# A layer's adaLN projection moved from TensorE to VectorE and TensorE together, and a bias table written in eight copies

## What is computed

```python
cond_act = jax.nn.silu(cond)
for i in range(DEPTH):
    mod = (cond_act @ ada_w[i] + ada_b[i])[:, None, :]      # ada_w[i]: 1024 x 6144
    sh1, sc1, g1, sh2, sc2, g2 = [mod[..., n * D:(n + 1) * D] for n in range(6)]
    h = rms_norm(x, norm1_g[i]) * (1 + sc1) + sh1
    # m = pool_mix / attention / fourier_mix of h
    x = x + g1 * m
    h = rms_norm(x, norm2_g[i]) * (1 + sc2) + sh2
    x = x + g2 * moe(h, ...)
```

## Time and profile before

| what | value |
|---|---|
| median of 3 runs | 1320.46 us |
| lowest and highest run | 1318.17, 1323.54 us |
| the profiled execution | 1320.7 us, of which the span is 1318.9 us |
| TensorE busy | 1247.3 us (95%) |
| VectorE busy | 392.1 us (30%) |
| ScalarE busy | 332.1 us (25%) |
| moved by DMA | 535.45 MB, 406 GB/s over the span |
| granted TensorE clock, mean | 0.983 |

### The profile page before, as it was taken

How to read it: one execution, slowest core, us unless ns; L and a number is a source line. 1 busy time by engine, 2 the same in 40 slices (tenths; PEclk the granted TensorE clock), 3 DMA queues, 4 the chain that set the end, 5 groups by cost and what they waited for, 6 DMA issues and landing times.

```text
span 1318.9 us, 17286 instructions
## 1 busy us (share of the span) xinstructions
PE 1247.3 (95%) x6581; PEld 563.0 (43%) x6581; DVE 392.1 (30%) x884; ACT 332.1 (25%) x714; POOL 37.7 (3%) x76
## 2 busy tenths in 40 slices
PE   3879999999899999999999899999999989999996
PEld 0434434343756644443434354443443454434342
DVE  1242213222232324221332324222231452213324
ACT  1141212122221223221212233221221452212122
POOL 2100000000200000000100000000000000000000
PEclk9879999999999999999999999999999999999998
DMA  9999999999999988999999999999999999999994
GB/s 371 420 420 421 421 421 421 421 420 421 398 368 409 394 335 360 422 421 421 420 420 421 421 407 399 422 421 421 420 421 421 415 421 418 422 420 420 422 420 182
DMA packets 87279, 535.45 MB, mean 406 GB/s; under 512 B 11192, under 2 KB 13336, under 8 KB 25760
## 3 DMA queue, kind: packets, MB, share of 16 engines
q1 hardware_dynamic: 82336, 527.47, 97.3%
q0 software_dynamic: 3120, 5.17, 1.1%
q10 hardware_dynamic: 1744, 1.73, 0.4%
HBM read 532.20 MB, written 2.12 MB: 405 GB/s over the span
## 4 chain that ended last, share of the span: by engine, by line
PE 86%; DMA 7%; DVE 4%; ACT 2%; issue 1%; SPq 0%; DVEq 0%; ACTq 0%
PE ps L1939 33%; PE ps L1988 15%; PE ps L1925 5%; PE ps L2000 5%; PE ps L1614 4%; PE ps L1451 4%; PE ps L1576 4%; DMA ring<-in_ada_w_dram 4%; PE ps L1971 3%; PE ps L1623 2%; DMA ring<-in_attn_wqkv_dram 2%; DMA ring<-in_moe_w_down_dram 2%; PE ps L1956 1%; PE ps L1548 1%; ACT hT L707 1%; PE ps L1485 1%
## 5 line engine op out<-in xcount | busy, mean ns | idle before, releaser
L1941 PE MATMUL ps<-ring,xg 128*64 128x512 f32 x968 | 438.0, 597 | 0.0
L1939 PE MATMUL ps<-ring,xg 128*64 128x512 f32 x912 | 412.5, 597 | 2.8 <-DMA ring<-in_moe_w_up_dram 2.8
L1988 PE MATMUL ps<-ring,gb 128*64 128x512 f32 x992 | 225.6, 595 | 0.3 <-DMA ring<-in_moe_w_down_dram 0.3
L1939 PEld LDWEIGHTS ps<-ring,xg 128*64 128x64 f32 x912 | 117.5, 137 | 228.4 <-issue 218.7
L1375 DVE SCALAR_TENSOR_TENSOR gb<-ps,gslot,g2x 128x512 f32<-128x512 f32 x128 | 90.2, 746 | 248.3 <-PE ps L1988 248.3
L1988 PEld LDWEIGHTS ps<-ring,gb 128*64 128x64 f32 x992 | 68.7, 137 | 134.4 <-issue 126.8
L1941 PEld LDWEIGHTS ps<-ring,xg 128*64 128x64 f32 x968 | 124.8, 136 | 0.0
L885 ACT ACTIVATE y_hi<-gb 128x512 fp32r<-128x512 f32 x128 | 77.1, 627 | 169.0 <-PE ps L2000 109.1
L1451 PE MATMUL ps<-ring,cact 128*32 128x512 f32 x768 | 93.0, 618 | 12.9 <-DMA ring<-in_ada_w_dram 7.2
L872 ACT ACTIVATE gu<-ps 128x512 f32<-128x512 f32 x64 | 38.3, 598 | 246.5 <-PE ps L1941 246.5
L1384 DVE TENSOR_TENSOR y_lo<-gb,y_hi 128x512 fp32r<-128x512 f32 x128 | 83.6, 688 | 12.5 <-ACT y_hi L885 11.9
(11 more groups left out here) (221 smaller groups left out, 1127.2 us busy)
## 6 DMA issues: line engine op xcount, KB each, us to landing
ring<-in_moe_w_down_dram SPq DMA_DIRECT2D x124, 1024.0 KB, 17.4
ring<-in_moe_w_up_dram SPq DMA_DIRECT2D x121, 1024.0 KB, 16.8
ring<-in_moe_w_gate_dram SPq DMA_DIRECT2D x114, 1024.0 KB, 17.3
ring<-in_ada_w_dram SPq DMA_DIRECT2D x96, 1024.0 KB, 17.7
ring<-in_attn_wqkv_dram SPq DMA_DIRECT2D x12, 1024.0 KB, 21.6
spare<-in_moe_w_down_dram SPq DMA_DIRECT2D x4, 1024.0 KB, 23.7
xh<-in_moe_w_up_dram SPq DMA_DIRECT2D x4, 1024.0 KB, 21.0
hT<-in_moe_w_gate_dram SPq DMA_DIRECT2D x4, 1024.0 KB, 22.5
```

Of the source, the lines that this page charges most:

```text
L1939: mg = pe.matmul(ps[0:SLOTS, B_GU, :], xg[:, b, e, :], wg[:, i * F:(i + 1) * F], start=(b == 0), stop=(b == DB - 1))
L1941: mu = pe.matmul(ps[SLOTS:P, B_GU, :], xg[:, b, e, :], wu[:, i * F:(i + 1) * F], start=(b == 0), stop=(b == DB - 1))
L1988: mm = pe.matmul(ps[r * SLOTS:(r + 1) * SLOTS, DOWN_BANKS[e % 2], :], acts[:, e % ACTS, j, :], w[:, i * D + r * HALF:i * D + (r + 1) * HAL ...
```

## The change

Third 7 is no longer done by TensorE's `ada`. VectorE multiplies each of its eight units by the conditioning of its 128 rows, one column of `cact` for each of the two sequences, and adds up the eight in two buffers of 128 x 2048 floats, `sums[0]` and `sums[1]` (`summed`, in the rows below `TENSOR_SCALAR` and `SCALAR_TENSOR_TENSOR` on `ring,cact`). TensorE then sums each buffer over its 128 partitions with four matrix products whose weights are a column of ones in a field of zeros (`reduce_sums`, eight products in all). The buffers are `spare` and the room of the first four head pairs' queries and keys, so `qT` and `kT` are laid out anew as `first_qk` and `second_qk`.

The eight units move in SP's order, the steps around them move in the engines' orders, and their slots are given back by VectorE through a semaphore of its own, `s_summed`. The second half of third 6 moves behind the eighth pair's scores on TensorE.

The bias table is held eight times in DRAM. After the first copy POOL's queue makes the others with three DMAs from DRAM to DRAM (1 to 2, 2 to 4, 4 to 8 copies). Copies lie 32 KB apart; neighbouring partitions of a load of `braw` read from different copies.

```diff
@@ BEFORE_EXPERTS[1]
-    + matrix_units("qkv", 4) + ada_units(5) + matrix_units("qkv", 1) + ada_units(6)[:4] + matrix_units("qkv", 3) + ada_units(6)[4:]
-    + matrix_units("qkv", 5) + ada_units(7) + matrix_units("wo", 0) + ada_units(8)[:4] + matrix_units("wo", 1) + ada_units(8)[4:],
+    + matrix_units("qkv", 4) + ada_units(5) + matrix_units("qkv", 1) + ada_units(7)[:1] + ada_units(6)[:4] + ada_units(7)[1:3]
+    + matrix_units("qkv", 3) + ada_units(7)[3:4] + matrix_units("qkv", 5) + ada_units(7)[4:6] + ada_units(6)[4:] + ada_units(7)[6:]
+    + matrix_units("wo", 0) + ada_units(8)[:4] + matrix_units("wo", 1) + ada_units(8)[4:],
@@ SP, room
-                    sp.wait_ge(s_used, used(USE_OF[at - RING], l, base))
+                    u = USE_OF[at - RING]
+                    if u in SUMMED_UNITS:
+                        sp.wait_ge(s_summed, NSEQ * SUMMED_UNITS[u])
+                    else:
+                        sp.wait_ge(s_used, used(u, l, base))
@@ POOL, the bias table
+            copied = 1
+            while copied < COPIES:
+                pool.wait_ge(s_bias, 32 + 16 * (copied.bit_length() - 1))
+                pool.dma_start(bias_dram[copied:2 * copied, 0:3], bias_dram[0:copied, 0:3]).then_inc(s_bias, 16)
+                copied *= 2
+            pool.wait_ge(s_bias, 16 * 5)
...
                     src = bass.AP(tensor=bias_dram.tensor, offset=((kr - r + 1) * P + 1) * HEADS,
-                                  ap=[[HEADS, GRID_W], [1, GRID_W * HEADS]])
+                                  ap=[[COPIES * HEADS, GRID_W // COPIES], [(4 * P + 1) * HEADS, COPIES], [1, GRID_W * HEADS]])
@@ VectorE
+            def summed(i, seqs=range(NSEQ)):
+                at = place(UNIT_AT[("ada", SUMMED, i)], 1)
+                w = ring[:, at % RING, :]
+                if 0 in seqs:
+                    v.wait_ge(s_slot[at % RING], landed(at, 1, bases[1]))
+                for s in seqs:
+                    if i == 0:
+                        ins = v.tensor_scalar(sums[s], w, cact[:, i, s:s + 1], None, ALU.mult)
+                    else:
+                        v.wait_ge(s_summed, NSEQ * (i - 1) + s + 1)
+                        ins = v.scalar_tensor_tensor(sums[s], w, cact[:, i, s:s + 1], sums[s], ALU.mult, ALU.add)
+                    ins.then_inc(s_summed, 1)
@@ VectorE, attention
                 normalise(3)
-                empty(Q1B, blocks(qT, 6, 2))
+                v.wait_ge(s_job, JOB_DONE[K_TURN0])
+                summed(0)
+                empty(Q1B, second(0, 2))
+                summed(1)
                 copy_output(2)
+                summed(2)
                 copy_output(3)
                 bias_max(4)
+                summed(3, [0])
                 normalise(4)
-                empty(K1B, blocks(kT, 6, 2))
+                empty(K1B, second(1, 2))
+                summed(3, [1])
                 bias_max(5)
+                summed(4, [0])
                 normalise(5)
-                ada_rows(6, l, base)
+                summed(4, [1])
                 bias_max(6)
+                summed(5, [0])
                 normalise(6)
-                ada_mods(6)
                 empty(V1B, vtok[:, 1, 512:1024])
+                summed(5, [1])
                 copy_output(4)
                 bias_max(7)
                 copy_output(5)
                 normalise(7)
                 copy_output(6)
+                ada_rows(6, l, base)
+                ada_mods(6)
                 copy_output(7)
+                summed(6)
+                summed(7)
                 ada_rows(7, l, base)
                 ada_mods(7)
@@ TensorE
+            def reduce_sums():
+                pe.wait_ge(s_mod, SUMMED)
+                pe.wait_ge(s_summing, 2)
+                pe.wait_ge(s_summed, NSEQ * ADA_UNITS)
+                for s in range(NSEQ):
+                    for j in range(4):
+                        mm = pe.matmul(ps[32 * j:32 * (j + 1), B_ADA, :], summing[:, 31 - s:63 - s], sums[s][:, j * 512:(j + 1) * 512],
+                                       start=(s == 0), stop=(s == NSEQ - 1))
+                mm.then_inc(s_reduced, 1)
@@ TensorE, attention
                 attend(5)
-                ada(7, 0, 6, l, base)
+                ada(6, 4, ADA_UNITS, l, base)
                 turn(7)
                 attend(6)
-                ada(7, 6, ADA_UNITS, l, base)
                 attend(7)
                 gates(l, 0)
-                ada_turn(7)
+                ada_turn(6)
                 pe.wait_ge(s_os, PAIRS)
-                project(l, base, "wo", oT, (4, 5, 6, 7), lambda: ada(8, 0, 4, l, base))
+                project(l, base, "wo", oT, (4, 5, 6, 7),
+                        {(0, 1, 0): reduce_sums, (0, 1, 1): lambda: ada_turn(7), (1, 0, 0): lambda: ada(8, 0, 4, l, base)})
```

More of the change, by code:

```diff
@@ L124 @@
 B_ADA = B_G
+SUMMED = 7
+SUMMED_UNITS = {UNIT_AT[("ada", SUMMED, i)]: i + 1 for i in range(ADA_UNITS)}
 TURNED_BANKS = [B_T, B_Y, B_G]
@@ L210, in used @@
 def used(u, l, base):
-    return base * NU + (u + 1 - LAYER_UNITS * l)
+    return base * NU + (u + 1 - LAYER_UNITS * l - sum(1 for of in SUMMED_UNITS if of <= u))
 def build(nc, x_prompt, x_sample, cache_k, cache_v, c, c_ctx, ada_w, ada_b, norm1_g, norm2_g, pool_w,
@@ L362, in build @@
         knew = ck
+        qT, kT = [[(first_qk, second_qk)[b // 4][:, i, b % 4, :] for b in range(DB)] for i in range(2)]
+        sums = [spare[:, :], first_qk[:, :, :, :].rearrange("p i b t -> p (i b t)")]
         ps = ctx.enter_context(nc.psum_tensor("ps", [P, 8, 512], F32))
-        bias_dram = nc.dram_tensor("bias_rows", [3, P, HEADS], F32, kind="Internal").ap()
+        bias_dram = nc.dram_tensor("bias_rows", [COPIES, 4, P, HEADS], F32, kind="Internal").ap()
         s_vec_in = sem("s_vec_in")
@@ L565, in group @@
                     u = EXPERTS_AT[l] + v
[L566 removed]
+                    sp.wait_ge(s_used, used(EXPERTS_AT[l], l, it) + (v - RING))
                     sp.sem_inc(s_issue, 1)
@@ L758, in blocks, with second, first @@
                     return of[:, b:b + n, :].rearrange("p d t -> p (d t)")
+                def second(i, b):
+                    return blocks(second_qk[:, i, :, :], b, 2)
+                def first(i, b):
+                    return blocks(first_qk[:, i, :, :], b, 2)
                 def exps(hp):
@@ L775, in copy_turned @@
                     nc.scalar.activation(pT[:, hp % 2, :, :], ps[:, 0:2, 0:3 * P], ACT.Copy).then_inc(s_pts, 1)
-                empty(Q0, blocks(qT, 0, 2))
-                empty(K0, blocks(kT, 0, 2))
+                empty(Q0, first(0, 0))
+                empty(K0, first(1, 0))
                 for n in range(2):
@@ L790, in attention @@
                 exps(2)
-                empty(Q1A, blocks(qT, 4, 2))
+                empty(Q1A, second(0, 0))
                 copy_turned(2)
@@ L795, in attention @@
                 copy_turned(3)
-                empty(K1A, blocks(kT, 4, 2))
+                empty(K1A, second(1, 0))
                 exps(4)
@@ L1107, in copy_output @@
                     v.tensor_copy(oT[hp], ps[:, 2, 0:T]).then_inc(s_os, 1)
-                empty(Q0 + 1, blocks(qT, 2, 2))
-                empty(K0 + 1, blocks(kT, 2, 2))
-                v.wait_ge(s_bias, 16 * 6)
+                empty(Q0 + 1, first(0, 2))
+                empty(K0 + 1, first(1, 2))
+                v.wait_ge(s_bias, 16 * 9)
                 flat = braw[:, :, :, :].rearrange("p r k h -> p (r k h)")
@@ L1561, in pool_tokens, with project @@
                               start=True, stop=True).then_inc(s_pm, 1)
-            def project(l, base, name, src, banks, between=None):
+            def project(l, base, name, src, banks, between):
                 for cc in range(2):
-                    if cc == 1 and between is not None:
-                        between()
                     for s in range(NSEQ):
-                        if (cc, s) == (0, 1):
-                            gates(l, 1)
-                        if cc == 1:
-                            pe.wait_ge(s_g2x, 2 * l + 2)
                         for h in range(2):
+                            if (cc, s, h) in between:
+                                between[cc, s, h]()
+                            if (cc, s, h) == (0, 1, 0):
+                                gates(l, 1)
+                            if cc == 1 and h == 0:
+                                pe.wait_ge(s_g2x, 2 * l + 2)
                             w = unit(UNIT_AT[(name, cc, h)], l, base)
@@ L1674, in attention @@
                 emptied(K0 + 1)
-                turned(K_TURN0, [kT[:, i, 0:SEQ] for i in range(4)])
+                turned(K_TURN0, [kT[i][:, 0:SEQ] for i in range(4)])
                 ada(4, 0, ADA_UNITS, l, base)
@@ L1726, in attention @@
                 scores(6)
-                turned(K_TURN1, [kT[:, 4 + i, 0:SEQ] for i in range(4)])
-                ada_turn(6)
+                turned(K_TURN1, [kT[4 + i][:, 0:SEQ] for i in range(4)])
                 by_token(V1B, w, 1)
```

(3 more changed lines are left out.)

27 lines of the change are left out of this document (17 added, 10 removed).

## The result

| | before | after |
|---|---|---|
| median of runs | 1321.45 us (1318.17 to 1323.61, 6 runs) | 1326.05 us (1324.73 to 1329.17, 6 runs) |
| ratio, 95% interval | | 1.0035 [1.0024, 1.0046] |
| profiled execution, span | 1320.7, 1318.9 us | 1324.7, 1322.9 us |
| VectorE busy | 392.1 us | 425.5 us |
| end of attention's projection | 512.58 us | 515.86 us |

The kernel became slower by 0.35%, where I had forecast 0.15% faster, and it lies outside my range. It is still within the 0.5% that I had called no change.

What follows compares the result with a forecast made beforehand. TensorE's chain was taken to bound attention up to the projection's end, with slack in the load stream. Terms -7.15 - 1.4 + 1.85 + 4.25 = -2.45, with copies +0.4, -2.05, gave 1318.5 us; 8-in-10 range 1313.5 to 1324.5.

Steps and rivals of the forecast that it cites:

- Bias table: Attention's `braw` loads: eight copies read at the stream's pace, removing V0's DMA wait, -1.4 us on TensorE's chain.
- Making the copies: Layer 0's full stream: copying moves 168 KB more, +0.4 us, with bounds of 0 and +2.
- The copies don't help: Rival, 13 in 100: the bias read stays slow, V0's wait stays, K1A waits 1.0; 1320.9 us, no change.
- -7.15 + 1.85 + 4.25: TensorE's chain in attention: third 7's eight units removed, eight reducing products added, five new waits added, in us.
- every two-source row keeps 1.0 ns a column: VectorE in attention, beside a full stream: argument against dear sums, supporting 2.3 us per 2048-column sum.
- The order of the loads: K1A's units stand three loads (7.5 us) later; with the bias gain they are 2.4 early, costing nothing.
- the first rival: The copies don't help, 13 in 100: V0's wait stays, K1A waits 1.0; 1320.9 us.
- The rule: What the end of attention's projection (512.6) moves by is what the kernel moves by.
- VectorE's sums are dear: Rival, 12 in 100: a sum takes 3.85 us, lengthening attention's waits; about 1333 us, slower.
- the new waits don't come: Rival, 8 in 100: sums overlap or TensorE's cover is longer; up to 4.25 us comes back, 1314.3.
- the stream is the bound in attention: Rival, 4 in 100: the 4.8 us of regained stream count in full; about 1314 us.

Runs made afterwards that it cites:

- t4: Kernel before, with the cache's two loads of 128 partitions cut into four of 64; 1328.29 us (one run).
- a6: Kernel before, with bias windows read from an input by two loads of 128 partitions, plain list of 128 rows (bias wrong); 1318.7 us, ratio 0.9959.
- a2: Kernel before, with each bias window load reading 64 separate aligned 4 KB rows of an input (bias wrong); 1321.69 us, ratio 1.0002.
- e2: Kernel before, with only the bias table held eight times; 1327.06 us, ratio 1.0038.
- a5: Kernel before, with bias windows read from input rows as 64-partition loads, source in three dimensions, 8 x 8 rows (bias wrong); 1325.92 us, ratio 1.0016.
- t2: Kernel before with the bias table held eight times, copies 36 KB apart in place of 32; 1327.59 us (one run).
- e1: Changed kernel with the bias table held once: VectorE's sums and the new order alone; 1321.61 us, ratio 0.9996 to the kernel before.
- e3: Changed kernel with one bias table, last output copied ahead of `ada_mods(6)`, sums reduced one projection block later; 1317.77 us, ratio 0.9976 to the kernel before.
- t7: e3 with the upper half's two window loads on ScalarE's queue and GpSimd's two ahead of the cache's; 1315.8 us, ratio 0.9959 to the kernel before.
- t1: Kernel before, with the four bias window loads made two of 128 partitions, source in three dimensions; 1346.39 us, ratio 1.0193.
- a3: Kernel before, with bias windows read from input rows 4160 B apart (bias wrong); 1324.28 us (one run).

## Why the prediction was wrong

**The step that failed** is "*Bias table.* If eight copies read at the stream's pace ... -1.4", with "Making the copies ... +0.4", and with it the price of the rival "The copies don't help". I had seen a slow stretch beside reads of one 8 KB place and taken the place for its cause, though the same rows fit the shape of the loads as well, and the fast loads of the cache right ahead of it differ in just that: 128 partitions against 64. t4 and a6 (404 GB/s against a2's 287) show the width to be the cause, with the load of `kpool` against the rival of size and number. The terms of -1.4 and +0.4, a gain of 1.0, came out as 4.33 us of loss at V0's end. The rival had the sign of a missing gain, but its price ended at a read as slow as the one of before. The change also gave the source a third dimension, with which the read was slower (e2, a5), and that case had no chance of its own.

**What it cost, along TensorE's chain**, in the profiled executions: attention's first product starts 1.04 us later (339.99 against 338.95). V0 waits 1.59 more, so it starts 2.63 later (381.88 against 379.25). It then takes 1.69 longer (8.80 against 7.11) because the clock fell behind the wait, and what follows V0 starts 4.33 later (390.52 against 386.19). From there to the end of the projection the change gains 1.05, and 3.28 remain.

The 1.04 at the start goes with the copies. A qkv load that SP issues at 312.84 in the kernel before leaves at 313.90, 313.64 and 313.74 in the three kernels with copies (changed, e2, t2), and at 312.61 to 313.00 in the twelve others. The copies are issued between 60 and 75 us. Whether their traffic costs this or the waits between them on GpSimd's queue, no run tells apart. The forecast had +0.4 for the traffic, with bounds of 0 and +2 that hold it.

**The sums** went by the forecast. Behind V0 I had -7.15 + 1.85 + 4.25 = -1.05; measured -1.05. Singly: `turn(7)` 0.28 (0.35), `attend(7)` 0.62 (0.6), the projection 0.90 (1.0), `reduce_sums` 1.93 (2.2), and `attend(5)` about 0.2 (0.3). These brackets are a little shorter than what the chain loses. From start to start, the projection begins 1.55 behind the turn ahead of it (478.86 and 477.31), where it began 0.49 behind (479.98 and 479.49): 1.06 net, where the sum has 0.8.

```profile
477.31 0.66 PE L1542 MATMUL ps<-const,rows 128*128 128x128 f32 x4
```

So the terms were each right to 0.3 us, and that their total agrees to the hundredth is luck. The Trainium skill (VectorE: DVE Perf Modes, section The perf-mode tier table) gives 2293 ns for the fp32 `tensor_tensor` of 2048 columns and 1227 for one-source operations. The trace, with its `SCALAR_TENSOR_TENSOR`, has 2345 and 1282. The forecast's claim that every two-source row keeps 1.0 ns a column passed over its own `braw` row (1.88); the sums came out at some 1.14. The reducing products took 1.86 us from 487.92 to 489.78 (1.85).

**The order of the loads**: the first rival had K1A wait 1.0 where the read isn't faster. e1 and e3 show 0.86 and 0.91. In the changed kernel V0's own delay hides it.

**The rule** that the kernel moves by what the projection's end moves by: +3.3 and +4.0 us of span here, +0.03 and +0.9 in e1, -3.0 and -3.1 in e3, +4.4 and +2.2 in e2. It holds to about 1 us, and to 2.2 in e2. The rest goes with stretches of some 3.4 us at half the clock that fall at different places from kernel to kernel. Behind attention the kernel before has them at 756 and 1087 us, the changed one at 532, 826 and 1092. e2 has none there, and its loads are 4.4 late up to 720, 3.8 from 829 to 1073 and 2.1 from 1180. That execution, 1322.84 us, is one of the two fastest of e2's ten, whose median is 1327.06. Which of them an execution gets, I can't predict.

**The other rivals**: "VectorE's sums are dear" fell with 2.34 us a sum, "the new waits don't come" with the waits above, and "the stream is the bound in attention" with a6's chain, where 404 GB/s gave 1.4 us at the projection's end and not 4.8 (its ratio alone wouldn't rule 4.8 out).

**The mechanism**, as far as pages reach. Loads into 64 partitions slow the traffic (t4, a6), and with two such loads in flight together it stays slow (307 GB/s in t7). The Trainium skill (SBUF — State Buffer, sections Door 1: The DMA port swizzle and "Can I just issue two DMAs to hit both halves?") states both: partitions 0 to 63 reach 8 of the 16 ports, and two transfers to the halves can't be fused. The trace agrees, with 307 GB/s in t4 and in t7 where loads of 128 partitions had 418. A source of three dimensions slowed the read little with 8 in the outermost and much with 2 (a5, t1). The Trainium skill (DMA: Bandwidth & Descriptors, section Rules for kernel authors) states that the outermost dimension's size, where it is under 16, bounds the number of engines that a load uses. The order of t1, a5 and a2 (2, 8 and 64 outermost; 51.8, 26.7 and 21.9 us to the last landing) agrees; no trace here names the engines that a load used, and no run has a third dimension with 16 or more outermost, which would tell the size from the third dimension as such. I should have weighed both pages before the prediction.

**Still open** is that last distinction, how much the eight regions of a5 add to it, and whether a load of 128 partitions can be had in a kernel that computes the reference, from a table written once more in 16 segments; it wasn't tried.

## What to carry to other kernels

When a stretch has fully busy DMA engines and moves too little, compare the shape of its loads (partitions written, dimensions of the source) with that of fast loads next to it before believing in a place in memory; here the fast row was 10 us away. A rival "it doesn't help" needs a bound on the other side too: ask what else the edit changes in the instruction, here a third dimension. And a wait of TensorE can cost more than its length, since the product behind it may run at half the clock; a new wait that has a few microseconds of other work within reach is better moved than accepted (e3).

## What the runs showed of the hardware

- Loads into 64 partitions of 4 KB in place of 128 took the whole traffic from 418 to 307 GB/s (t4 against before) and from 404 to 287 (a2 against a6), with the DMA engines' share at 1.01 to 1.04 throughout.
- A source of three dimensions: 8 x 8 rows of 4 KB, in eight regions, took the last landing from 21.9 to 26.7 us (a5 against a2) with 64 packets more per load; 2 x 64 rows took it from 17.8 to 51.8 us, with 896 packets more per load (t1 against a6, both two loads of 128 partitions; a6's places differ).
- A 256 KB load into 128 partitions left the stream at 418 GB/s (`kpool`, kernel before).
- In the changed kernel the granted clock was 0.50, the 1.2 GHz level, over 382.2 to 385.5, behind a wait of 3.00, and the product of 7.11 us took 8.80. In a3 it took 8.80 behind a wait of 1.73, and in e1 it took 7.11 behind a wait of 2.71, so the length of the wait alone doesn't decide it.
